# Turning both halves of the probabilities behind the scores of the next step, in the attention part of a decoder layer

## The reference

```
h = rmsnorm(x);  proj = h @ w_in
A: 3 groups (window, dilation) = (128,1), (512,4), (2048,16), 4 heads of 64;
   banded softmax attention in each, outputs merged by their softmax denominators
B: 8 query heads over 2 key heads of 64, window 128, a learned sink in the denominator
M: 4 heads of 128 over 256 memory tokens (k, v from rmsnorm(mem) @ w_mem_kv), full softmax
gates = sigmoid(h @ w_gate + b_gate);  merged = sum of gate_i * (o_i @ w_o_i)
x = x + merged @ w_out;  x = x + conv_ffn(rmsnorm(x))
```

## Time and profile before

| | us |
|---|---|
| median of 3 runs | 1746.8 (1746.7, 1746.8, 1753.89) |
| the profiled execution | 1753.89, of which the span is 1752.1 |
| PE matmul busy | 1681.4 (96% of the span) |
| DVE busy | 848.1 (48%) |
| ACT busy | 634.4 (36%) |
| POOL busy | 865.3 (49%) |
| projections and attention | from 0 to about 588 of the span |

### The profile page before, as it was taken

How to read it: one execution, slowest core, us unless ns; L and a number is a source line. 1 busy time by engine, 2 the same in 40 slices (tenths; PEclk the granted TensorE clock), 3 DMA queues, 4 the chain that set the end, 5 groups by cost and what they waited for, 6 DMA issues and landing times.

```text
span 1752.1 us, 22400 instructions
## 1 busy us (share of the span) xinstructions
PE 1681.4 (96%) x8625; PEld 1381.5 (79%) x8625; DVE 848.1 (48%) x1242; ACT 634.4 (36%) x1135; POOL 865.3 (49%) x671
## 2 busy tenths in 40 slices
PE   5999999999899899999999999899999999999999
PEld 4887878778677688888888787788888888788887
DVE  6555243457874112200155247788888888522101
ACT  5455565545544222222111323434343334322110
POOL 6543656533322122222144566999999998222221
PEclk9999999999999799999999999999999999999999
DMA  6113011110110233332355711222232223443411
GB/s 214 37 58 100 1 37 40 37 45 13 43 37 1 61 111 97 96 97 84 116 166 165 247 51 48 90 79 73 84 95 74 73 84 101 164 144 132 144 48 60
DMA packets 131253, 151.05 MB, mean 86 GB/s; under 512 B 16780, under 2 KB 97356, under 8 KB 131148
## 3 DMA queue, kind: packets, MB, share of 16 engines
q1 hardware_dynamic: 131148, 149.63, 26.9%
HBM read 116.98 MB, written 32.62 MB: 85 GB/s over the span
## 4 chain that ended last, share of the span: by engine, by line
PE 61%; DVE 2%; POOL 2%; DMA 1%; ACT 1%; issue 0%; SPq 0%; DVEq 0%; ACTq 0%; POOLq 0%
PE ps L2341 23%; PE ps L1694 15%; PE ps L2426 13%; PE ps L1710 6%; PE ps L1726 3%; DMA w_raw<-in_w_out_dram 1%; POOL wo L1587 1%; POOL f_lo L2182 0%; PE ps L1719 0%; DVE ffn_area L2299 0%; DVE attn_lo L2291 0%; DVE t_all L2209 0%; ACT wo L1518 0%; DVE ffn_area L1679 0%; DVE attn_out L2244 0%
## 5 line engine op out<-in xcount | busy, mean ns | idle before, releaser
L2182 POOL TENSOR_TENSOR f_lo<-ffn_area,f_hi 128x1024 fp32r<-128x1024 f32 x85 | 201.8, 2394 | 20.5 <-ACT f_hi L2069 20.5
L2341 PE MATMUL ps<-t_all,f_hi 128*128 128x512 f32 x528 | 164.1, 392 | 2.0 <-DVE t_all L2209 1.6
L1592 POOL TENSOR_TENSOR g_lo<-g_raw,g_hi 128x1024 fp32r<-128x1024 f32 x23 | 55.3, 2406 | 208.5 <-ACT g_hi L1502 208.5
L1694 PE MATMUL ps<-act_hi,g_hi 128*128 128x512 f32 x384 | 152.4, 397 | 3.4 <-DVE g_lo L1627 3.4
L2214 POOL TENSOR_TENSOR attn_lo<-ffn_area,attn_lo 128x512 fp32r<-128x512 f32 x44 | 58.6, 1331 | 194.3 <-ACT attn_lo L2131 194.3
L1694 PE MATMUL ps<-act_hi,g_lo 128*128 128x512 f32 x384 | 151.3, 394 | 0.0
L1694 PE MATMUL ps<-act_lo,g_hi 128*128 128x512 f32 x384 | 150.0, 391 | 0.0
L2069 ACT ACTIVATE f_hi<-ffn_area 128x1024 fp32r<-128x1024 f32 x85 | 80.2, 946 | 187.9 <-PE ps L2341 177.5
L2341 PE MATMUL ps<-act_hi,f_hi 128*128 128x512 f32 x336 | 133.1, 396 | 4.6 <-POOL f_lo L2182 4.6
L2341 PE MATMUL ps<-act_hi,f_lo 128*128 128x512 f32 x336 | 132.5, 394 | 0.0
L1229 PE MATMUL ps<-w_hi,act_hi 128*128 128x512 f32 (+1 forms) x320 | 123.0, 384 | 9.2 <-DVE act_lo L476 4.1
(11 more groups left out here) (258 smaller groups left out, 4257.8 us busy)
## 6 DMA issues: line engine op xcount, KB each, us to landing
ffn_area<-in_w_up_dram SPq DMA_DIRECT2D x44, 512.0 KB, 5.2
gates<-gate SPq DMA_DIRECT2D x24, 512.0 KB, 3.1
gate<-gates SPq DMA_DIRECT2D x24, 512.0 KB, 3.9
g_raw<-in_w_gate_dram SPq DMA_DIRECT2D x23, 512.0 KB, 4.6
z<-attn_out SPq DMA_DIRECT2D x22, 512.0 KB, 2.6
ffn_area<-in_w_down_dram SPq DMA_DIRECT2D x22, 512.0 KB, 4.2
ffn_area<-z SPq DMA_DIRECT2D x44, 256.0 KB, 3.0
attn_out<-in_x_dram SPq DMA_DIRECT2D x16, 512.0 KB, 6.0
```

The lines of the kernel that those rows point to most:

```text
L1592: pool.tensor_tensor(g_lo[:, n % 3], g_raw[:, n % 2], g_hi[:, n % 3].bitcast(F32), ALU.subtract).then_inc(g_lo_done, 1)
L1694: ins = pe.matmul(ps[:, u % 4, :], w[:, n % 3, k, :], a[:, k, HALF[half]], start=(k == 0 and i == 0), stop=(k == NK - 1 and i == 2))
L2182: pool.tensor_tensor(part_place(p, part, f_lo, first_lo), part_source(p, part), part_place(p, part, f_hi, first_hi).bitcast(F32), ALU.subt ...
L2341: ins = pe.matmul(out, w, a, start=(start and k == 0 and i == 0), stop=(stop and k == 3 and i == 2))
```

## The change

It alters where the pieces of a step stand in the streams of PE, ACT and DVE, and nothing of what they compute. Both turns of step n-1 now stand behind `score(n)` and `weigh_values(n-2)`: unit 0 one slice behind them and unit 1 three slices (B), or two and four slices (A, M). The copies on ACT move with them, so both now stand behind `exps(n)`. The twelve `merge_use` of DVE go to other slices, and to the end of their slice, behind `divide`, `normalise`, `copy_k` and `w_low` of the same slice.

```diff
-SECOND_TURN = {1: 3, 0: 2, 4: 6}
-def second_turns(j):
-    return {SECOND_TURN[step]: i for i, step in enumerate(step_slices(j))}
+TURNS_BEHIND = {1: (3, 5), 0: (1, 3), 4: (5, 7)}
+def prob_turns(j):
+    return {k: (u, i) for i, step in enumerate(step_slices(j)) for u, k in enumerate(TURNS_BEHIND[step])}
...
-        MERGE_AT = [(merge_from + d, k) for d, k in ((2, 0), (2, 4), (3, 4), (4, 4), (5, 4), (6, 4), (7, 4),
-                                                     (8, 1), (8, 5), (8, 7), (9, 1), (9, 5))]
+        MERGE_AT = [(merge_from + d, k) for d, k in ((2, 2), (2, 6), (3, 2), (4, 2), (5, 2), (6, 2), (7, 2),
+                                                     (8, 2), (8, 4), (8, 6), (9, 2), (9, 4))]
...  ACT
                     if k in step_slices(j):
-                        n = steps_before(j) + step_slices(j).index(k)
-                        at(copy_probs, n - 1, 0)
-                        at(exps, n)
-                    if k in second_turns(j):
-                        at(copy_probs, steps_before(j) + second_turns(j)[k] - 1, 1)
+                        at(exps, steps_before(j) + step_slices(j).index(k))
+                    if k in prob_turns(j):
+                        u, i = prob_turns(j)[k]
+                        at(copy_probs, steps_before(j) + i - 1, u)
...  DVE, after minima and copy_out
-                    if (j, k) in MERGE_AT:
-                        merge_use(MERGE_AT.index((j, k)))
...  DVE, at the end of the slice
+                    if (j, k) in MERGE_AT:
+                        merge_use(MERGE_AT.index((j, k)))
...  PE
                             n = steps_before(j) + step_slices(j).index(k)
-                            at(turn_probs, n - 1, 0)
                             at(score, n)
                             at(weigh_values, n - 2)
-                        if k in second_turns(j):
-                            at(turn_probs, steps_before(j) + second_turns(j)[k] - 1, 1)
+                        if k in prob_turns(j):
+                            u, i = prob_turns(j)[k]
+                            at(turn_probs, steps_before(j) + i - 1, u)
```

## The result

The changed kernel takes 1758.4 us in the median of four runs (1757.2, 1757.8, 1759.1, 1759.5), the kernel before 1747.2. The ratio is 1.0054, with a 95% interval of 1.0032 to 1.0077: slower by 9.4 us (5.6 to 13.5), 11.2 by the medians. The forecast was 1748.5, so the time lies inside the range (1740 to 1759), near its upper end. The direction was right; the size was six times too small (+1.55 against +9.4).

What follows compares the result with a forecast made beforehand. PE was taken as the bound, its matmuls busy 1681.4 of 1752.1 us. The terms -2.9 - 1.5 + 1.0 + 0 + 4.35 + 2.5 - 1.9 sum to +1.55, on the median 1746.8: 1748.5 us, range 1740 to 1759.

Steps and rivals of the forecast that it cites:

- points 1 and 2: B's undisturbed rounds 30, 32 to 34: unit 0's waits removed, -2.9 us; round 31: shorter wait, -1.5 (0 to -4).
- point 3: Rounds 33 and 34: merges now behind the first half's divide make the next minima late, +1.0 us (0 to +3).
- both come some 0.6 earlier: Rounds 33 and 34: first half's divide and next scores both end about 0.6 us earlier, divide still 0.9 ahead.
- The spare of 1.0: Second half of a round of B: unit 0's copy is ready 1.0 us before PE reaches unit 1's turn.
- point 4: Rounds 35 to 37, border from B to M: 8.5 us of waits removed, 9.0 new; counted as 0 (-4 to +4).
- point 5: Borders of A and the memory, rounds 8, 9, 19, 20, 27 and 28: later copies and turns, +4.35 us (+1 to +7).
- Point 6: Rounds 38 to 40 of M: unit 1's turn waits for a copy behind late minima, +2.5 us (0 to +5).
- Point 7: The end, rounds 44 to 46: scores start first, the last value product comes earlier, -1.9 us (-4 to +1).
- the copy is late everywhere, or the borders cost twice: Rival: unit 1's turn waits for late copies throughout, 1761 us, or borders cost double; chance 0.15, 0.16 above 1755.5 with forecast's tail.
- The waits go and stay away: Rival: copies never late, waits mostly in B and its borders vanish, 16.3 us won, 1730.5 us; chance some 0.13.

Runs made afterwards that it cites:

- B's turns alone: Kernel before with the new places of turns and copies in rounds 30 to 37 only, merges at old places: 1740.1 us, ratio 0.9944.
- turns alone: The changed kernel with the twelve merges back at their old places, turns and copies at the new ones: 1751.7 us, ratio 1.0018.
- M and the end alone: Kernel before with the new places of turns and copies in rounds 38 to 46 only, merges at old places: 1751.4 us, ratio 1.0012.
- turns alone, copy between: Changed kernel with merges at old places and unit 0's copy between the exponentials of unit 0 and unit 1: 1740.0 us, ratio 0.9949.
- A and the memory alone: Kernel before with the new places of turns and copies in rounds 0 to 29 only, merges at old places: 1756.8 us, ratio 1.0042.
- B's turns and the copy between: Kernel before with new turn places in rounds 30 to 37 only, unit 0's copy there between both units' exponentials, merges at old places: 1737.6 us, ratio 0.9934.
- the kernel with rounds 44 to 46: Kernel before with new turn places and unit 0's copy between the exponentials in rounds 30 to 37 and 44 to 46, merges at old places: 1737.8 us, ratio 0.9943.

## Where the prediction was right, and where not

Its main mechanism was right. The waits for `divide` went (forecast under 4 us, none left); the waits for ACT's copy rose to 27.2 (12 or more); unit 1's turn waits for a copy queued behind the exponentials; rounds 30 and 32 have no wait. One sign failed: the longest wait was to be in round 36, 4 to 7 us, and is 3.06, in round 44, where none was named.

The sum of +1.55 stands against +9.4. That the time came inside the range is due to the width of the range, 19 us, and not to the terms: but for points 1 and 2 they all erred to the same side. Up to the gates the traces show 6.7 us of loss (6.0, and the 0.7 by which the first scores are earlier); which part of the code has the rest of the 9.4 no trace shows, and the interval (5.6 to 13.5) takes in both.

1. *Undisturbed rounds and round 31 (points 1 and 2).* Forecast -4.4, by the trace of B's turns alone -3.7 and -1.4. Right to 0.7. Nearly all of that is about 0.2 us more in each undisturbed round than its wait; that this is the switching, which I had counted as the same, is not shown.

2. *Merges in rounds 33 and 34 (point 3).* Forecast +1.0, measured +2.7 (1.33 in each round between the traces with and without the merges). The failed step is "both come some 0.6 earlier". Only the scores do: the divide hangs on the scores of the first half, and its end stays 7.0 us behind their end (431.74 to 438.73 before; 435.38 to 442.36 after), while the time from one scores to the next shrank from 7.92 to 7.07. So the divide ends 0.1 us before the scores, not 0.9, and the minima are 2.27 late instead of 1.3. The spare of 1.0 was right: 2.27 less the wait of 1.09 is 1.18. The rule of the Trainium skill ("GPSIMD Engine Reference", "1. Specifications") would have made this point +2.6, which is nearly the number measured, but not by its way: the merge beside POOL took 2.37 us against 2.20, and not 0.8 more.

3. *Rounds 35 to 37 (point 4).* Forecast 0, measured +0.4 in the changed kernel, and that is luck. Of the single waits only some were right: 2.16 in round 35 (forecast 1.6); in round 36, where I had one of 6.0, there are three, 1.62 ahead of the scores for the copy of the keys, 0.29, and 2.57 in the second half. And the point held two terms in one, which cancelled: the turns alone gain about 3 us here, the merges cost about 4.

4. *Borders (point 5).* Forecast +4.35, measured +7.3 for the stage; rounds 8 to 10 are 6.4 of it, where I had 2.25. This is the mis-sized term. I priced how much later the turn of the queries is, by counting from a copy that ends at 130.98, and that count came near the waits: 1.99 and 1.94 us, where I had 1 to 2.3, but 2.46 in round 20, and 2.37 in round 28, where I had named none. I gave no price to the clock behind them, some 1.5 us each time, though I had done so for round 36.

5. *M and the end (points 6 and 7).* +2.5 and -1.9 forecast, +2.6 and -1.1 by the two traces, +2.1 (-0.7 to +4.7) together by the runs. Point 6 was right in the changed kernel (round 39 waited 2.17); with the merges at their old places M loses 4.2 (turns alone) and 4.7 us (M and the end alone) by the traces. Point 7 failed in its mechanism. I had the last value product start 1.9 us earlier; it starts 24.0 us behind the scores of round 44 (591.57), where it had started 23.3 behind them (583.86 in the earlier trace rows), because unit 1's turn now waits 3.06 and 1.98 us for the copy. What was won is that it took 2.05 us, not the 3.78 of half clock. The new order need not have given that: from the scores of round 44 to the first gate product the eight traces with the old places there take 27.1 to 30.5 us, the three with the new ones 29.2 to 29.5.

The rival "the copy is late everywhere, or the borders cost twice" (1761, 0.16) is nearer to the time than my forecast. By its mechanism only its second half is: in B the copy is late only where other work of DVE holds up the minima (the merge factors in round 31, the merges in 33 to 36, and in 35 and 36 the next stage's weights). "The waits go and stay away" comes nearest in B's rounds, with the merges at their old places: 9.8 us won, with one wait above 2 us for the copy left, in round 31.

## What to carry to other kernels

Before a wait is moved, look at which queue its result comes from: two turns that share a bank make the second one wait for a copy. Behind four exponentials that copy was late (19.5 us of waits); between them it came earlier (10.3) and the kernel won; ahead of them, tried with the merges moved, the waits turned up again at the keys and the scores. Price each stage of a change by itself, since the same edit won 9.8 us in one and lost 7.3 in another. And when one engine is sped up, the work that hangs on its *previous* result does not move with it: the cover of whatever stands in between shrinks by just the gain.

## What the runs showed of the hardware

Behind a single wait of PE the granted clock was halved in some executions and not in others, and between 1.4 and 2.9 us the length of the wait does not tell which. The wait of round 28, in the changed kernel and in the one with turns alone, and the 4 us from its end in each:

```profile
355.13 0.41 PE L1301 MATMUL ps<-ident,prob 128*128 128x128 f32 x2 [2.37 <-ACT prob_t L826]
355.13:359.13 4.00, 4.00 (x30) 3.80 (x31) 0.65 (x2) 1.76 (x5) 0.48 (x2) 1.00 0.00 0
```
```profile
350.85 0.41 PE L1301 MATMUL ps<-ident,prob 128*128 128x128 f32 x2 [2.33 <-ACT prob_t L826]
350.85:354.85 4.00, 4.00 (x22) 4.00 (x23) 0.42 (x1) 0.77 (x2) 0.49 (x2) 0.59 0.00 0
```

The next scores came 13.18 us behind those of round 28 in the first and 14.77 in the second, so the half clock cost 1.6 us. The same happened with one code: at the same turn of the queries the kernel before waited 2.00 us in one execution, with 0.62 behind it, and 1.92 in the other, with 1.00, and took 1.6 us less. Further out, a wait of 1.40 for the memory's values was followed by 0.60 (turns alone, copy between) and one of 2.86 for the copy in round 20 by 1.00 (A and the memory alone). The wait of about 4.1 us in round 36 had 0.50 behind it in all five traces that have it. Two waits of 1 us close together, at the end of round 36 and the start of round 37, were enough in the kernel with B's turns and the copy between:

```profile
472.88 0.30 PE L1265 MATMUL ps<-ident,qk 128*128 128x128 f32 x1 [1.02 <-issue]
...
474.99 2.08 PE L1301 MATMUL ps<-k_ring,q_ring 64*128 64x128 f32 x16 [1.04 <-issue]
```

and in the kernel with rounds 44 to 46 as well the same two, of 1.02 and 1.05 us, had a clock of 1.00 behind them (scores at 1.16). So the same code loses about 1.6 us or does not, from one execution to the next. The Trainium skill ("TensorE: Matmul & The Clock Gate", "What's actually happening") says that the clock is halved by default and that activity releases it; the traces agree in that the half clock here stood behind idle time of PE (0.66 and 0.58 in the stretches behind waits of 2 us). It does not settle which of these waits bring it.

POOL and DVE held each other up where a merge met the rotation: POOL's last operation took 1.44 us beside the merge, where it had taken 0.52, and the merge 2.37 against 2.20. POOL's operation before, then after:

```profile
438.66 0.52 POOL L702 TENSOR_TENSOR qk<-rope_a,rope_b 128x160 f32<-128x160 f32 x1
```
```profile
442.29 1.44 POOL L702 TENSOR_TENSOR qk<-rope_a,rope_b 128x160 f32<-128x160 f32 x1
```
